# The MLP's second projection waits for each inner tile at the contraction step that reads it, not for all 16 at once

## The chip, the cores and the metric

The kernel runs on one core of a Trainium2 chip. The metric is device time in microseconds (us), the median of three runs. The profiles come from one profiled execution. A core has five engines with their own instruction queues, which are kept in order among each other by semaphores alone: TensorE (PE in the profile, its weight loads PEld), VectorE (DVE), ScalarE (ACT), GpSimd (POOL), and SyncE (SP), which here only issues transfers.

## What is computed

The reference runs one inference step of a 4-layer decoder trunk on 512 prompt tokens and 8 sampled tokens. Each layer has a token mixer (HGRN2, sparse attention, S5, and HGRN2 again) and then a squared-ReLU MLP, each followed by a LayerNorm over the scaled residual. Cut to the MLP, a layer is:

```
FFN_HIDDEN = 4 * D_MODEL          # 1024 -> 4096 -> 1024
def sq_relu_mlp(x, w1, w2):
    return jnp.square(jax.nn.relu(x @ w1)) @ w2
...
xp = layer_norm(DN_ALPHA * xp + mp, ln_mix_g[i], ln_mix_b[i])
xp = layer_norm(DN_ALPHA * xp + sq_relu_mlp(xp, mlp_w1[i], mlp_w2[i]), ln_ffn_g[i], ln_ffn_b[i])
```

The sampled tokens go through the same layers. All arrays are fp32.

## The kernel before

**Layout.** Activations are stored transposed: features on the 128 partitions, the 520 tokens (512 + 8) along the free dimension, in tiles of 128 features by 520 tokens. x has 8 such tiles. Every dense layer is cut into *chunks*: one chunk is a 1024 x 128 block of a weight matrix, that is 8 contraction steps (k) of 128 x 128. To keep fp32 accuracy each operand is split into a high and a low part (x into xh and xl, a weight into wh and wl), and each product is made of three: high by high, low by high, high by low (lines L1476, L1477, L1478 in the function `chunk`). As 520 tokens don't fit one bank of PSUM, each step is done for two halves of 260 tokens. A chunk is thus 8 x 2 x 3 = 48 matmuls of 128*128 by 128x260, each with its own weight load.

**The weight stream.** The weights of the whole program are one stream of 389 chunks. SP loads chunk n into `raw` (2 slots), ACT copies it to `wh` (4 slots, L546 or L554), POOL subtracts to get `wl` (L350) and raises `w_low`. ACT may make the wh of chunk n once PE has finished chunk n-4 (`chunk_done`), so three chunks lie ready ahead of the one in work. In layer 0 the mixer has 40 chunks (numbers 0 to 39); its MLP begins with chunk 40.

**The MLP of a layer** is done in two halves of 16 hidden tiles (HHALF = 16). In each half:

- *First projection*: 16 chunks, one per hidden tile. PE accumulates tile T in one of two PSUM places (`lp`, T % 2). ACT applies ReLU out of PSUM into `lw` (L934, `tile_out`), DVE squares it (L1448), rounds it to the high part `hh` (L1449), and subtracts to get the low part `hl` (L1450). That last one raises `h_ready`, one per hidden tile. `h_ready` counts over the program, and g1 is its value when this half begins.
- *Second projection*: 8 output tiles, each of two chunks (b = 0 and 1), which contract over the 8 hidden tiles 8b to 8b+7. So chunk b reads at step k hidden tile 8b + k. After the second chunk of a tile DVE takes the sum out of PSUM into the residual `r` (L981 in the first half, L979 in the second).

Both projections are loops (`Fori`) of four chunks a pass on PE, except that the first four chunks of the first half are written out, as their steps wait for x tile by tile. The order of instructions on each engine is that of the code. After the second half `stats` (L1505) sums the residual for the LayerNorm (ones_mean).

**Waits on PE at the switch.** Between the two projections PE has one wait, at L1852, for `h_ready >= g1 + 16`: all 16 hidden tiles. Ahead of each tile it waits until the PSUM place is emptied (`tile_out >= T - 1`, the tile before the last), and ahead of each chunk for `w_low`. There are 4 layers x 2 halves = 8 such switches in the program.

Of the kernel before, what the change touches and what calls it, by code (L numbers as in the profile page):

```python
# [26 lines left out]
KT = D // P  # L27
# [8 lines left out]
HHALF = HID // 2 // P  # L36
# [19 lines left out]
SPL = 4  # L56
# [46 lines left out]
def trunk(nc, I, O, kinds=KINDS):  # L103
# [3 lines left out]
    def sb(name, shape, dt=F32, c=ctx):  # L107
        return c.enter_context(nc.sbuf_tensor(name, shape, dt))

    def sem(name):  # L110
        return ctx.enter_context(nc.semaphore(name))
# [29 lines left out]
    hh = sb("hh", [P, HHALF, N], F32R, c)  # L141
    hl = sb("hl", [P, HHALF, N], F32R, c)
# [77 lines left out]
    w_high, w_low, chunk_done = sem("w_high"), sem("w_low"), sem("chunk_done")  # L220
    tile_out = sem("tile_out")
    h_ready = sem("h_ready")
# [1237 lines left out]
    def _(pe):  # L1460
        def bank(T, half):
            b = 2 * (T % 2) + half
            return lp[:, b, 0:NH2]

        def chunk(n, slot, T, hi, lo, k0, start, stop, split=None, ks=range(KT)):

            if 0 in ks:
                pe.wait_ge(w_low, n + 1)
            for k in ks:
                if split is not None:  # L1470
                    pe.wait_ge(xl_ready, split + k + 1)
                w = slice(k * P, (k + 1) * P)
                for half in range(2):
                    t = slice(half * NH2, (half + 1) * NH2)
                    first, last = start and k == 0, stop and k == KT - 1
                    pe.matmul(bank(T, half), wh[:, slot, w], hi[:, k0 + k, t], start=first, stop=False)  # L1476
                    pe.matmul(bank(T, half), wh[:, slot, w], lo[:, k0 + k, t], start=False, stop=False)  # L1477
                    ins = pe.matmul(bank(T, half), wl[:, slot, w], hi[:, k0 + k, t], start=False, stop=last)  # L1478
            return ins

        def tile(n, T, split=None):

            if T >= 2:
                pe.wait_ge(tile_out, T - 1)
            chunk(n, n % SPL, T, xh, xl, 0, True, True, split).then_inc(chunk_done, 1)

        def part(n, T, ks, split=None):

            if 0 in ks and T >= 2:
                pe.wait_ge(tile_out, T - 1)  # L1490
            ins = chunk(n, n % SPL, T, xh, xl, 0, True, True, split, ks)
            if KT - 1 in ks:
                ins.then_inc(chunk_done, 1)

        def pair(n, T, split, ks=range(KT)):

            for k in ks:
                part(n, T, (k,), split)
                part(n + 1, T + 1, (k,), split)
# [235 lines left out]
        for y in plan:  # L1735
# [96 lines left out]
            for half in range(2):  # L1832
                c1, t1 = y["cm"] + 32 * half, y["tm"] + 24 * half
                s0_ = 0
                if half == 0:

                    pair(c1, t1, 8 * (3 * y["i"] + 2))
                    s0_ = 1
                g1 = HHALF * (2 * y["i"] + half)
                if half == 0:  # L1840
                    for c in range(2, 4):
                        tile(c1 + c, t1 + c)
                    lo_, hi_ = 1, HHALF // 4
                else:
                    lo_, hi_ = 0, HHALF // 4
                with pe.Fori(lo_, hi_) as i:
                    for c in range(4):
                        T = t1 + c
                        pe.wait_ge(tile_out, i * 4 + T - 1)
                        chunk(i * 4 + (c1 + c), (c1 + c) % SPL, T, xh, xl, 0, True, True).then_inc(chunk_done, 1)  # L1850
                c2, t2 = c1 + HHALF, t1 + HHALF
                pe.wait_ge(h_ready, g1 + HHALF)  # L1852
                with pe.Fori(0, KT // 2) as i:
                    for m in range(2):
                        T = t2 + m
                        pe.wait_ge(tile_out, i * 2 + T - 1)
                        for b in range(2):
                            n = c2 + 2 * m + b
                            ins = chunk(i * 4 + n, n % SPL, T, hh, hl, 8 * b, b == 0, b == 1)
                            ins.then_inc(chunk_done, 1)  # L1860
# [137 lines left out]
```

## Time and profile before

| what | value |
|---|---|
| median of 3 runs | 3756.96 us (3751.52 to 3760.11) |
| profiled execution, first to last instruction (span) | 3748.7 us |
| PE busy | 3153.9 us, 84% of the span |
| DVE, POOL, ACT busy | 1876.3, 1489.6 and 1120.3 us |
| PE's share of the chain that ended last | 65% |

The profiled execution has no time of its own taken outside the chip's profiler; its span lies 8.3 us below the median of the runs, which also hold the start and the end of the execution. TensorE's granted clock has two levels in this trace: 1.00 of full speed (2.4 GHz) and half of it (1.2 GHz); a value between is a stretch that holds both. In the rows a matmul's end is modelled and neighbours overlap, so the pace is read from start to start.

### The profile page before, as it was taken

How to read it: one execution, taken by the hardware profiler on the slowest of the kernel's cores; microseconds unless marked ns; L12 is line 12 of the kernel's file. 1: busy time of each engine (PE TensorE's matmuls, PEld its weight loads, DVE VectorE, ACT ScalarE, POOL GpSimd, SP SyncE). 2: the span in 40 equal slices, each digit the busy share in tenths (PEclk: the TensorE clock that was granted, in tenths of full speed). 3: DMA queues.
4: the chain of work that ended last, by engine and by line, in shares of the span. 5: the costliest groups of instructions: out<-in, count | busy, mean ns of one | idle time of the engine just before them, and what ended most of it. 6: DMA issues, size and time to landing. Idle time of an engine off the chain costs nothing.

```text
span 3748.7 us, 56136 instructions
## 1 busy us (share of the span) xinstructions
PE 3153.9 (84%) x22360; PEld 2861.9 (76%) x22360; DVE 1876.3 (50%) x2586; ACT 1120.3 (30%) x1827; POOL 1489.6 (40%) x837
## 2 busy tenths in 40 slices
PE   7889689998799788999555667899998888689998
PEld 7888689998589578999511114799998888689997
DVE  4666654252170326233489996460615655754152
ACT  3433332223322223222223222331224433342222
POOL 4222263445233035344345555543443222254443
PEclk9888799999789679999767778999998887899999
DMA  3211122322424212222200000222222212122221
GB/s 113 69 58 58 35 81 85 94 84 68 100 80 155 94 52 79 84 90 84 71 3 1 0 0 12 79 90 84 90 84 72 65 57 58 41 79 85 90 84 68
DMA packets 104309, 260.23 MB, mean 69 GB/s; under 512 B 9587, under 2 KB 44915, under 8 KB 103763
## 3 DMA queue, kind: packets, MB, share of 16 engines
q1 hardware_dynamic: 56592, 206.10, 17.5%
q10 hardware_dynamic: 42434, 34.07, 3.3%
q0 software_dynamic: 5120, 17.83, 1.3%
q8 instruction: 110, 1.80, 0.2%
q14 instruction: 53, 0.43, 0.0%
HBM read 239.09 MB, written 18.88 MB: 69 GB/s over the span
## 4 chain that ended last, share of the span: by engine, by line
PE 65%; DVE 16%; issue 7%; ACT 6%; POOL 3%; DMA 1%; ACTq 1%; DVEq 0%; POOLq 0%; SPq 0%
PE lp L1476 18%; PE lp L1478 17%; PE lp L1477 17%; PE mb L1548 4%; DVE ph L1381 2%; DVE lw L1030 2%; DVE rot L1353 2%; POOL lw L474 1%; DVE lw L1027 1%; DVE dd L1096 1%; PE lp L1705 1%; DVE qt L994 1%; DVE lw L1362 1%; PE mb L1559 1%; PE mb L1648 1%
## 5 line engine op out<-in xcount | busy, mean ns | idle before, releaser
L350 POOL TENSOR_TENSOR wl<-raw,wh 128x1024 fp32r<-128x1024 f32 x389 | 959.6, 2468 | 1449.8 <-ACT wh L554 834.3
L1476 PE MATMUL lp<-xh,wh 128*128 128x260 f32 x4176 | 1238.7, 297 | 101.9 <-POOL xl L360 94.0
L1478 PE MATMUL lp<-xh,wl 128*128 128x260 f32 x4176 | 1212.4, 290 | 0.0
L1477 PE MATMUL lp<-xl,wh 128*128 128x260 f32 x4176 | 1210.8, 290 | 0.0
L1476 PEld LDWEIGHTS lp<-xh,wh 128*128 128x128 f32 x4176 | 823.6, 197 | 115.5 <-issue 79.3
L1477 PEld LDWEIGHTS lp<-xl,wh 128*128 128x128 f32 x4176 | 822.3, 197 | 0.5
L1478 PEld LDWEIGHTS lp<-xh,wl 128*128 128x128 f32 x4176 | 821.2, 197 | 0.0
L1476 PE MATMUL lp<-hh,wh 128*128 128x260 f32 x2048 | 589.1, 288 | 41.0 <-DVE hl L1450 41.0
L1478 PE MATMUL lp<-hh,wl 128*128 128x260 f32 x2048 | 587.6, 287 | 0.0
L1477 PE MATMUL lp<-hl,wh 128*128 128x260 f32 x2048 | 585.9, 286 | 0.0
L1476 PEld LDWEIGHTS lp<-hh,wh 128*128 128x128 f32 x2048 | 395.6, 193 | 42.6 <-POOL wl L350 42.6
L1477 PEld LDWEIGHTS lp<-hl,wh 128*128 128x128 f32 x2048 | 394.9, 193 | 0.0
L1478 PEld LDWEIGHTS lp<-hh,wl 128*128 128x128 f32 x2048 | 394.7, 193 | 0.0
L1791 PE MATMUL lp<-ph,r 128*32 128x512 f32 x256 | 182.5, 880 | 172.9 <-DVE ph L1381 156.5
L1450 DVE TENSOR_TENSOR hl<-lw,hh 128x520 f32 x128 | 315.0, 2461 | 16.4 <-DVE hh L1449 1.2
L546 ACT ACTIVATE wh<-raw 128x1024 fp32r<-128x1024 f32 x192 | 202.7, 1056 | 346.0 <-PE lp L1478 310.6
L1791 PEld LDWEIGHTS lp<-ph,r 128*32 128x32 f32 x256 | 36.2, 154 | 311.2 <-issue 151.7
L554 ACT ACTIVATE wh<-raw 128x1024 fp32r<-128x1024 f32 x197 | 207.1, 1051 | 216.2 <-PE lp L1478 136.7
L981 DVE SCALAR_TENSOR_TENSOR r<-x,lp 128x520 f32<-128x520 f32 x56 | 39.0, 696 | 461.9 <-PE lp L1478 461.8
L1548 PE MATMUL mb<-qt,kt 128*128 128x64 f32 x896 | 171.8, 359 | 106.0 <-ACT tok L692 106.0
L1548 PEld LDWEIGHTS mb<-qt,kt 128*128 128x128 f32 x896 | 169.6, 281 | 109.5 <-issue 109.5
L934 ACT ACTIVATE lw<-lp 128x520 f32<-128x520 f32 x128 | 77.6, 606 | 493.2 <-PE lp L1478 488.9
(307 smaller groups left out, 3713.7 us busy)
## 6 DMA issues: line engine op xcount, KB each, us to landing
raw<-in_wstream SPq DMA_DIRECT2D x389, 512.0 KB, 3.5
s<-in_s_in ACTq DMA_DIRECT2D x16, 512.0 KB, 4.1
out_hg_s<-s ACTq DMA_DIRECT2D x16, 512.0 KB, 3.3
pg<-in_kpages POOLq DMA_DIRECT2D x16, 512.0 KB, 5.7
pg<-in_vpages POOLq DMA_DIRECT2D x16, 512.0 KB, 5.4
bias_rows<-bsm ACTq DMA_DIRECT2D x1, 2560.0 KB
x<-in_xT ACTq DMA_DIRECT2D x4, 520.0 KB, 7.9
out_kT<-r ACTq DMA_DIRECT2D x1, 2080.0 KB, 11.4
```

Source lines behind the costliest of these rows:

```text
L350: pool.tensor_tensor(wl[:, s, :], raw[:, r_, :], wh[:, s, :].bitcast(F32), ALU.subtract).then_inc(w_low, 1)
L546: act.activation(wh[:, s, :], raw[:, r_, :], ACT.Copy).then_inc(w_high, 1)
L554: act.activation(wh[:, n % SPL, :], raw[:, n % RAW, :], ACT.Copy).then_inc(w_high, 1)
L934: act.activation(halves(lw[:, 6 + c % 2, :]), lp[:, 2 * (T % 2):2 * (T % 2) + 2, 0:NH2], ACT.Relu).then_inc(tile_out, 1)
L1030: dve.tensor_tensor(lw[:, 6 + m % 2, :], lw[:, 6 + m % 2, :], rstd, ALU.mult).then_inc(norm_ready, 1)
L1353: dve.tensor_tensor(rot[:, s, a, P:NP_].rearrange("p (a b) -> p a b", b=P), spun[:, 2 * a], spun[:, 2 * a + 1], (ALU.subtract, ALU.add)[a] ...
L1450: dve.tensor_tensor(lo, hq, hi.bitcast(F32), ALU.subtract).then_inc(h_ready, 1)
L1476: pe.matmul(bank(T, half), wh[:, slot, w], hi[:, k0 + k, t], start=first, stop=False)
L1477: pe.matmul(bank(T, half), wh[:, slot, w], lo[:, k0 + k, t], start=False, stop=False)
L1478: ins = pe.matmul(bank(T, half), wl[:, slot, w], hi[:, k0 + k, t], start=False, stop=last)
L1548: ins = pe.matmul(mb[:, 2 if l % 2 else 3, q2], kt[:, l - 1, ct[c]], qt[:, l - 1, q2], start=True, stop=True)
L1791: ins = pe.matmul(lp[f, 1 + k % 2, :], cmat[:, a, t, :], ph[:, t % 2, b, :], start=n == 0, stop=n == 3, tile_position=(0, 32 * (t % 4)))
```

## The change

`chunk` gets an argument `hidden`: where it is given, step k first waits for `h_ready >= hidden + k0 + k + 1`, that is for the hidden tile that it reads (k0 = 8b). The wait for all 16 goes. The first two output tiles of each half (four chunks) are written out ahead of the loop, the first of them with these waits and the second without (hidden=None), and the loop runs over the other six, in three passes.

```diff
-        def chunk(n, slot, T, hi, lo, k0, start, stop, split=None, ks=range(KT)):
+        def chunk(n, slot, T, hi, lo, k0, start, stop, split=None, ks=range(KT), hidden=None):
 
             if 0 in ks:
                 pe.wait_ge(w_low, n + 1)
             for k in ks:
                 if split is not None:
                     pe.wait_ge(xl_ready, split + k + 1)
+                if hidden is not None:
+                    pe.wait_ge(h_ready, hidden + k0 + k + 1)
                 w = slice(k * P, (k + 1) * P)
...
                 c2, t2 = c1 + HHALF, t1 + HHALF
-                pe.wait_ge(h_ready, g1 + HHALF)
-                with pe.Fori(0, KT // 2) as i:
+                for m in range(2):
+                    T = t2 + m
+                    pe.wait_ge(tile_out, T - 1)
+                    for b in range(2):
+                        n = c2 + 2 * m + b
+                        chunk(n, n % SPL, T, hh, hl, 8 * b, b == 0, b == 1, hidden=None if m else g1).then_inc(chunk_done, 1)
+                with pe.Fori(1, KT // 2) as i:
```

No matmul is added, removed or reordered in what is executed, and the programs of DVE, ACT, POOL and SP are the same as before. The first place is PE's program at the switch in the first half of layer 0. In the rows L1846 is the loop of the first projection (L1848 in the changed kernel, whose lines lie two further), L1853 the loop of the second, and in brackets stand the semaphores waited for. Before:

```order
L1478 MATMUL lp<-xh,wl 128x260
L1846 REGISTER_ALU
L1846 COMPARE_AND_BRANCH
L1853 UNCONDITIONAL_BRANCH [waits h_ready]
L1853 ISA
L1468 ISA [waits tile_out]
L1476 MATMUL lp<-hh,wh 128x260 [waits w_low]
L1477 MATMUL lp<-hl,wh 128x260
```

The same place in the changed kernel:

```order
L1480 MATMUL lp<-xh,wl 128x260
L1848 REGISTER_ALU
L1848 COMPARE_AND_BRANCH
L1478 MATMUL lp<-hh,wh 128x260 [waits h_ready,w_low,tile_out]
L1479 MATMUL lp<-hl,wh 128x260
L1480 MATMUL lp<-hh,wl 128x260
L1478 MATMUL lp<-hh,wh 128x260
L1479 MATMUL lp<-hl,wh 128x260
L1480 MATMUL lp<-hh,wl 128x260
L1478 MATMUL lp<-hh,wh 128x260 [waits h_ready]
```

The branch into the second loop and the wait for all 16 tiles are gone from between the projections; the first matmul now waits for the first hidden tile, and each following step (every sixth row) for its own. The second place is where the written-out tiles end and the loop of the second projection begins (L1860 in the changed kernel), four chunks later; before, these rows ran on inside the loop.

```order
L1478 MATMUL lp<-hh,wh 128x260
L1479 MATMUL lp<-hl,wh 128x260
L1480 MATMUL lp<-hh,wl 128x260
L1860 UNCONDITIONAL_BRANCH
L1860 ISA
L1468 ISA [waits tile_out]
L1478 MATMUL lp<-hh,wh 128x260 [waits w_low]
```

The branch into the loop now stands between two chunks, with no wait for the hidden tiles ahead of it. PE's program has 1536 more matmuls in its code (8 switches x 4 chunks x 48), with their weight loads; as the loops make one pass less, as many are executed as before.

## Rows read from the trace of the kernel before

**Rows 1.** The page: busy time, share of the span, instructions; granted clock in 40 slices
```profile
span 3748.7 us, 56136 instructions
PE 3153.9 (84%) x22360; PEld 2861.9 (76%) x22360; DVE 1876.3 (50%) x2586; ACT 1120.3 (30%) x1827; POOL 1489.6 (40%) x837
PEclk9888799999789679999767778999998887899999
```

**Rows 2.** The page's costliest groups: busy us, mean ns; idle before, and releaser
```profile
L1476 PE MATMUL lp<-hh,wh 128*128 128x260 f32 x2048 | 589.1, 288 | 41.0 <-DVE hl L1450 41.0
...
L1476 PEld LDWEIGHTS lp<-hh,wh 128*128 128x128 f32 x2048 | 395.6, 193 | 42.6 <-POOL wl L350 42.6
```

**Rows 3.** The list of waits: us in total, times, longest us
```profile
PE lp L1476 <- DVE hl L1450: 41.0, 8, 5.1
```

**Rows 4.** The timeline at the first switch: start us, us, idle before and releaser
```profile
619.08 0.28 PE L1478 MATMUL lp<-xh,wl 128*128 128x260 f32 x1
619.47 0.60 ACT L934 ACTIVATE lw<-lp 128x520 f32<-128x520 f32 x1 [4.18 <-PE lp L1478]
...
620.11 0.70 DVE L1448 TENSOR_TENSOR lw<-lw 128x520 f32<-128x520 f32 x1 [1.66 <-ACT lw L934]
620.95 0.43 DVE L1449 CAST hh<-lw 128x520 f32 x1
...
621.50 2.63 DVE L1450 TENSOR_TENSOR hl<-lw,hh 128x520 f32 x1
...
624.49 0.58 PE L1476 MATMUL lp<-hh,wh 128*128 128x260 f32 x1 [5.14 <-DVE hl L1450]
```

**Rows 5.** Windows of PE: us, busy us (matmuls), granted clock, DMA share, GB/s
```profile
619.08:624.49 5.41, 0.27 (x3) 0.93 0.28 97
624.49:638.82 14.33, 14.33 (x96) 0.79 0.17 55
...
2719.31:2724.71 5.40, 0.28 (x4) 0.84 0.29 95
2724.71:2738.58 13.87, 13.87 (x97) 0.82 0.20 46
3435.04:3440.44 5.40, 0.28 (x4) 0.94 0.27 95
3440.44:3454.79 14.35, 14.35 (x97) 0.79 0.17 47
```

**Rows 6.** Windows of PE: 15 chunks in mid-loop, and long stretches of one layer's MLP
```profile
719.18:805.28 86.10, 86.10 (x722) 1.00 0.29 91
...
631.00:814.00 183.00, 180.20 (x1507) 1.00 0.28 89
...
524.80:911.50 386.70, 373.57 (x3064) 0.98 0.28 87
```

**Rows 7.** POOL's low parts of weights that had started by 619.1 us
```profile
L350 POOL TENSOR_TENSOR wl<-raw,wh 128x1024 fp32r<-128x1024 f32 x59 | 146.2, 2479 | 336.6 <-ACT wh L554 296.3 <-ACT wh L546 40.2
```

**Rows 8.** PE's timeline: written-out code into a loop, a loop into a loop
```profile
550.20 0.28 PE L1478 MATMUL lp<-xh,wl 128*128 128x260 f32 x1
550.31 0.28 PE L1476 MATMUL lp<-xh,wh 128*128 128x260 f32 x1
...
719.06 0.28 PE L1478 MATMUL lp<-hh,wl 128*128 128x260 f32 x1
719.18 0.28 PE L1476 MATMUL lp<-xh,wh 128*128 128x260 f32 x1
```

**Rows 9.** PE's timeline: a loop into written-out code, and a step with met waits
```profile
910.57 0.28 PE L1478 MATMUL lp<-hh,wl 128*128 128x260 f32 x1
910.69 0.82 PE L1505 MATMUL mb<-lw,ones_mean 128*128 128x260 f32 x3
...
537.75 0.28 PE L1478 MATMUL lp<-xh,wl 128*128 128x260 f32 x1
537.87 0.28 PE L1476 MATMUL lp<-xh,wh 128*128 128x260 f32 x1
```

**Rows 10.** The page's DMA queues: packets, MB, time as a share of 16 engines' span
```profile
q8 instruction: 110, 1.80, 0.2%
```

## The prediction

> **What bounds the kernel now.** I read the page first. PE is busy 84% of the span, and no other engine over half of it [rows 1]. Busy PE is no proof that PE bounds the MLP, so I looked at the long stretches there: in 183 us in the middle of the first layer's MLP the clock is 1.00 throughout, and 15 chunks in the loop take 86.10 us, 5.74 us each or 0.12 us a matmul from start to start, without a gap [rows 6]. In that stretch ACT, POOL and DVE have their chunk's work done and wait for PE. So any time in which PE stands still in the MLP is lost to the span.
>
> The costliest groups then say where it stands still: the 2048 matmuls that begin a step on hh have 41.0 us of idle time before them, released by DVE's hl [rows 2]. The list of waits gives the same as 8 waits of at most 5.1 us, one for each switch [rows 3]. The timeline shows one of them [rows 4]. The last matmul of the last hidden tile starts at 619.08. ACT's ReLU, DVE's square, the rounding and the subtraction follow one after the other, and the subtraction ends at 621.50 + 2.63 = 624.13. PE's next matmul starts at 624.49, 5.41 us after the last one, where 0.12 is the pace. The 0.36 us at the end is semaphore and the branch into the loop.
>
> The reader should see a second loss, which no list of waits shows. After the stall the matmuls run slower: the next two chunks (96 matmuls) take 14.33 us, with a granted clock of 0.79, and two chunks at full pace take 2 x 5.74 = 11.48 [rows 5, 6]. The clock fell to its lower level during the stall, and PE runs the first part of the second projection at it.
>
> **The change, part by part.**
>
> *The wait for 16 tiles goes.* At the switch the first chunk needs hidden tiles 0 to 7 and the second, step by step, 8 to 15. Tile 15 is ready 624.13 - 619.08 = 5.05 us after PE's last matmul starts. PE comes to the step that reads it (k = 7 of the second chunk) after 15 steps of 6 matmuls: 15 x 6 x 0.12 = 10.8 us. Tile 14 was one chunk earlier in everything, so it is ready at about 624.13 - 5.74 = 618.4, before the switch. So each of the 16 new waits is met when PE gets there, the tightest with 10.8 - 5.05 = 5.7 us to spare; DVE's chain would have to more than double before anything is late. What lies beside PE's work is then the same ReLU, square, rounding and subtraction as before. That saves the gap: the eight are 5.41 us once and 5.40 seven times (to 0.01) [rows 5], 43.2 in all, less 8 x 0.12 for the pace, so 42.2 us.
>
> *The clock.* Without the stall, PE goes from one dense stretch into another. In the same trace it goes from the second projection of the first half into the first projection of the second at 719.06 to 719.18, and the clock stays at 1.00 [rows 6, 8]. So I take it that the clock doesn't fall at the switch. The 96 matmuls after the eight stalls took 13.87 to 14.35 us (the shortest and two of the longest are shown [rows 5]); all eight add up to 112.8 us, against 8 x 11.48 = 91.8. That is 21.0 us more to save. The bounds are 0 (the clock falls all the same) and 21.0.
>
> *PSUM and weights, the other two waits at the switch.* Tile t2 needs hidden tile 14 out of PSUM; its ReLU came one chunk before that of tile 15, so at about 613.7. Tile t2 + 1 needs that of tile 15, done at 619.47 + 0.60 = 620.07, when PE is in the first tile until 619.2 + 11.5. Weights: POOL has begun 59 low parts by 619.1 [rows 7], chunks 0 to 58, the last at 615.4, which ends after 2.5 us. The second projection begins with chunk 56; so 56, 57 and 58 are ready, and nothing comes of this wait. The price is 0.
>
> *The new waits as instructions.* A step whose wait is met costs nothing that can be seen: in the first pair of chunks, the second chunk's step at 537.87 waits for an xl tile which the chunk beside it had already used, and starts 0.12 us after its neighbour [rows 9]. Each chunk and each tile in the loop also has waits, and the pace is 5.74 us over 15 of them. I take 0. The upper bound is one start per wait, 16 x 8 x 0.12 = 15 us.
>
> *Written-out code in place of one pass of the loop.* Three seams are exposed now: loop into written-out code, written-out code into the loop, and a longer program to fetch. The first kind costs nothing at 910.57 to 910.69, the second nothing at 550.20 to 550.31, and a loop into a loop nothing at 719.06 to 719.18 [rows 8, 9]. Instructions come in 110 transfers of 16 KB (1.80 MB), whose time is 0.2% of 16 engines' span [rows 10]: 0.002 x 16 x 3748.7 / 110 = 1.1 us each. I take 0, as they run beside 5.74 us chunks; three of them exposed at every switch would be 8 x 3 x 1.1 = 26 us, the upper bound.
>
> The Trainium skill has a rule against this part ("Runtime: NRT & Kernel Launch", section "Instruction fetch mechanics"): a taken branch whose target isn't in the two pages held makes the engine wait for the page to come by DMA. By it, the branch into the second loop, which stood behind the long wait, would now stall PE once a switch, and the sum would shrink; the loop entries of this trace don't show such a stall.
>
> *The sum.* Saved 42.2 + 21.0 = 63.2 us, paid 0. The profiled execution's span of 3748.7 becomes 3685.5. It lies 8.3 us below the median of the runs, which I take over: 3756.96 - 63.2 = 3693.8 us, 1.7% less. DVE takes each output tile out of PSUM right after its second chunk, POOL and ACT are paced by PE's chunks; all move forward with PE, 15.8 us a layer, and the LayerNorm begins that much earlier.
>
> **The rivals.**
>
> *A. The clock falls all the same.* The lower clock could come from the change of operands or from long work instead of the idle time. For it: it follows every switch. Against it: at the switch back, at 719 us, it doesn't fall [rows 6, 8]. Then only the gaps are saved: 3756.96 - 42.2 = 3714.8.
>
> *B. Another wait takes the stall's place, so the change doesn't do what it says.* For it: the weight load at the same place has 42.6 us of idle time put down to POOL's wl, more than the 41.0 of DVE [rows 2]. If chunk 56 really waited for weights, PE would stand as long as before: 3757. Against it: the wl that ended within the stall is that of chunk 59, as 59 others had begun before it [rows 7]; it is named only because it ended last before the release.
>
> *C. Fetching shows.* Three transfers at every switch, 26 us: 3693.8 + 26 = 3720. For it is only that the program grows; the seams [rows 8, 9] speak against it.
>
> *D. Slower: full clock isn't granted for so long.* The longest stretch at 1.00 that I read is the 183 us between two stalls [rows 6]. The MLP of a layer would now be one dense stretch of 386.7 - 15.8 = 371 us. If the stalls are what gives the chip relief, the clock would fall within it. One slow spell costs what one after a stall does, 21.0 / 8 = 2.6 us. The layer gains 15.8 us, so from the seventh spell in a layer on (one every 53 us or closer) the kernel is slower; ten a layer give 3693.8 + 4 x 10 x 2.6 = 3798 us. For it is only that no longer stretch is seen; against it, that the clock is 1.00 right up to the stall after 183 us, with no spell on the way.
>
> The Trainium skill ("TensorE: Matmul & The Clock Gate", the section on the HAM clock gate) names a limiter for the current, which comes with a third busy core of a die and never with one or two. By that rule D falls away here, where one core works; no row of this trace goes beyond the 183 us.
>
> **How the numbers follow.** The forecast has 0.84, A 0.05, B 0.03, C 0.05, D 0.03. The likeliest case has a width of its own: the three runs differ by 8.6 us, 4.3 to each side; and where PE stalls elsewhere (19 of the page's 40 slices have a clock under 9 tenths [rows 1]), everything now comes at other moments, and the clock may return earlier or later, by the 0.5 us between the longest and shortest of the eight [rows 5] in each of the 19, 9.5 us to one side at the most. That is 3680 to 3708. To hold 8 in 10 with A within it I go to 3716. What a measurement can tell from no change is about 0.2%, 7.5 us. Forecast, A and C are faster by more: 0.94; B is no change: 0.03; D slower: 0.03.
>
> **What would show it.** Right, if: the list of waits has no L1478 on hh that waits for DVE's hl; in layer 0 the first matmul on hh starts 0.12 us after the last on xh, at about 619.2; the windows of the next 96 matmuls are 11.48 us at 1.00; the second half's first matmul comes at 719.2 - 7.9 = 711.3; and the clock is 1.00 from 525 us to about 895. A is right if those windows are 14 us after a gap of nothing. B, if the gap is there with POOL or ACT as its releaser. C, if gaps of a microsecond or more stand at L1478 behind the loops, released by nothing. D, if the clock falls in mid-stretch. I'd be wrong most likely in what lies outside the MLP, where I moved everything by 15.8 us a layer and took its length as unchanged.

## The result and the profile after

The changed kernel takes 3694.69 us (median of 4 runs, 3690.57 to 3700.71) against 3755.82 us for the kernel before (4 runs). The ratio is 0.9845 with a 95% interval of 0.9832 to 0.9859. The prediction was 3693.8 us. In the profiled executions the span goes from 3748.7 to 3688.8 us, 59.9 less.

The page's lines that answer to [rows 1, 2, 10]:

```profile
span 3688.8 us, 56096 instructions
PE 3137.7 (85%) x22360; PEld 2847.6 (77%) x22360; DVE 1869.1 (51%) x2586; ACT 1120.4 (30%) x1827; POOL 1491.1 (40%) x837
...
q8 instruction: 123, 2.02, 0.2%
...
L1478 PE MATMUL lp<-hh,wh 128*128 128x260 f32 x2048 | 578.3, 282 | 0.0
...
L1478 PEld LDWEIGHTS lp<-hh,wh 128*128 128x128 f32 x2048 | 385.4, 188 | 0.0
```

PE executes the same 22360 matmuls and is busy 16 us less: 19.5 us less in the four MLPs, where fewer of them run at the lower clock, and 3.3 us more outside them. The idle time ahead of the matmuls on hh was 41.0 us and is 0.0. The 42.6 us that the weight loads at the same place had put down to POOL's wl are gone too. That count belonged to the same stall.

The timeline at the first switch, against [rows 4]:

```profile
623.40 0.28 PE L1480 MATMUL lp<-xh,wl 128*128 128x260 f32 x1
623.52 0.28 PE L1478 MATMUL lp<-hh,wh 128*128 128x260 f32 x1
...
625.83 2.69 DVE L1450 TENSOR_TENSOR hl<-lw,hh 128x520 f32 x1
...
634.30 0.28 PE L1478 MATMUL lp<-hh,wh 128*128 128x260 f32 x1
```

PE goes on after 0.12 us. DVE finishes the last hidden tile at 628.52, beside PE's work. The step that reads this tile begins at 634.30, 5.8 us later. The windows that answer to [rows 5, 6], with length, busy time, matmuls and granted clock:

```profile
623.52:635.01 11.49, 11.49 (x98) 1.00 0.34 105
807.23:818.72 11.49, 11.49 (x98) 1.00 0.33 106
3391.74:3403.23 11.49, 11.49 (x98) 1.00 0.35 110
529.20:907.90 378.70, 370.69 (x3075) 1.00 0.28 89
719.18:805.28 86.10, 86.10 (x722) 1.00 0.29 92
```

Two chunks after a switch take 11.49 us, where they took 13.87 to 14.35. In the first layer the clock is 1.00 from 529.2 us to the end of the MLP at 899.09; only the MLP's first 14 matmuls, right behind the LayerNorm, run at the lower clock, as they did before (run 9). From the fifth chunk of each of the four MLPs on, where its first loop begins, no matmul starts more than 0.13 us after the one ahead of it, the entries into the loops included.

**Where the rest of the difference lies.** The first matmul of the sums for a LayerNorm (ones_mean) marks where a mixer and where an MLP ends. From one such mark to the next, an MLP with the LayerNorm ahead of it took 400.4, 400.3, 405.9 and 400.5 us before and takes 384.5, 384.6, 390.8 and 384.5 now, 62.7 us less in all. All that stands outside these four stretches (mixers, the LayerNorms ahead of them, and the last sums) took 2.8 us more, and 59.9 is left. These are the marks of the first layer: the first row is from the kernel before (its second mark is the 910.69 of [rows 9]), the other two are from the changed kernel.

```profile
510.25 1.91 PE L1505 MATMUL mb<-lw,ones_mean 128*128 128x260 f32 x8
...
514.58 0.60 PE L1507 MATMUL mb<-lw,ones_mean 128*128 128x260 f32 x2
...
899.09 0.38 PE L1507 MATMUL mb<-lw,ones_mean 128*128 128x260 f32 x1
```

Up to 510 us the two kernels have the same instructions on every engine, and yet the changed one's execution was 4.3 us late there. Run 8 looks into whether that is chance. Take these 4.3 us off, and the times named ahead came as written: the first matmul on hh at 623.52 (619.2 forecast), the second half's first matmul at 715.37 (711.3), and the end of the MLP at 899.09 (895).

### The profile page after: what moved, and what is told of

Same layout as the page of the kernel before. It is cut to its first block, busy times and chain, and to the rows that moved or that the text cites. A ratio compares the mean times of both kernels' runs of the same rounds, so it can differ in the third digit from the quotient of the medians.

```text
span 3688.8 us, 56096 instructions
## 1 busy us (share of the span) xinstructions
PE 3137.7 (85%) x22360; PEld 2847.6 (77%) x22360; DVE 1869.1 (51%) x2586; ACT 1120.4 (30%) x1827; POOL 1491.1 (40%) x837
## 4 chain that ended last, share of the span: by engine, by line
PE 65%; DVE 15%; issue 7%; ACT 6%; POOL 3%; DMA 2%; ACTq 1%; DVEq 0%; POOLq 0%; SPq 0%
PE lp L1478 18%; PE lp L1480 17%; PE lp L1479 17%; PE mb L1550 4%; DVE ph L1381 2%; DVE lw L1030 2%; DVE rot L1353 2%; POOL lw L474 1%; DVE lw L1027 1%; DVE dd L1096 1%; PE lp L1707 1%; DVE qt L994 1%; DVE lw L1362 1%; PE mb L1561 1%; PE mb L1507 1%
## 5 line engine op out<-in xcount | busy, mean ns | idle before, releaser
L1480 PE MATMUL lp<-hh,wl 128*128 128x260 f32 x2048 | 578.7, 283 | 0.0
L1478 PE MATMUL lp<-hh,wh 128*128 128x260 f32 x2048 | 578.3, 282 | 0.0
L1479 PE MATMUL lp<-hl,wh 128*128 128x260 f32 x2048 | 576.7, 282 | 0.0
L1478 PEld LDWEIGHTS lp<-hh,wh 128*128 128x128 f32 x2048 | 385.4, 188 | 0.0
L1480 PEld LDWEIGHTS lp<-hh,wl 128*128 128x128 f32 x2048 | 385.2, 188 | 0.0
L1479 PEld LDWEIGHTS lp<-hl,wh 128*128 128x128 f32 x2048 | 385.1, 188 | 0.0
```

## The experiments

Every kernel was timed beside runs of the kernel before on the same chip, so each ratio is to that kernel. Its medians were 3751.99 us beside runs 1, 2, 3 and 5, 3754.23 beside runs 4, 6, 7 and 8, and 3753.42 beside run 9.

**1. Fill the stall, keep the wait.** The kernel before, with extra matmuls ahead of its wait; they compute nothing that is used.

```diff
+                pe.wait_ge(w_low, c2 + 1)
+                for _ in range(42):
+                    pe.matmul(mb[:, 0, 0:NH2], wh[:, c2 % SPL, 0:P], xh[:, 0, 0:NH2], start=True, stop=True)
                 pe.wait_ge(h_ready, g1 + HHALF)
                 with pe.Fori(0, KT // 2) as i:
```

> The kernel before, with its wait for all 16 hidden tiles and its loops, but with 42 extra matmuls of 128*128 by 128x260 at each switch, ahead of that wait (8 x 42 = 336, into a PSUM bank that nothing reads at that time; the outputs are the same). At 0.12 us each they fill 5.0 of the 5.3 us in which PE stands still, so PE's useful work resumes no earlier than before. Theory (the idle time lowers the clock, and the clock's part is worth 21.0 us): the gap stays, the next 96 matmuls take 11.5 us at 1.00, and the time is 3756 - 21 = 3735 us. Rival (the clock falls with the switch of operands or after long work, idle or not): the 96 matmuls keep their 14.1 us and the time stays at 3756. Second rival (some of the 63 us came from the written-out code or its place in the loops): then nothing can be said of it here, as the loops are those of before.

Measured: 3738.49 us, ratio 0.9969 (0.9956 to 0.9983). The windows of its first two switches, gap and then 96 matmuls:

```profile
622.72:628.18 5.46, 5.26 (x45) 1.00 0.26 92
628.18:639.78 11.60, 11.60 (x96) 1.00 0.22 55
811.88:817.36 5.48, 5.27 (x46) 1.00 0.28 96
817.36:828.96 11.60, 11.60 (x97) 1.00 0.20 55
```

PE still goes on with hh 5.5 us after its last matmul on xh, but the chunks behind run at 1.00, at all eight switches. So the clock falls because PE stands idle, not because of the operands or the length of the work. That settles rival A. By the marks, the four MLPs are 19.3 us shorter than in the first profile of the kernel before, and 17.1 shorter than in its second one (run 8). The ratio shows 11.6 us (0.31% of the 3752), with an interval of 6.4 to 16.5. In the profiled execution 7.4 us more lay outside the MLPs; two profiles of the kernel before differ by 4.0 us there, and whether chance or the fillers put the rest there stays open.

**2. Write the code out, keep the wait.**

```diff
                 c2, t2 = c1 + HHALF, t1 + HHALF
+                pe.wait_ge(h_ready, g1 + HHALF)
                 for m in range(2):
...
-                        chunk(n, n % SPL, T, hh, hl, 8 * b, b == 0, b == 1, hidden=None if m else g1).then_inc(chunk_done, 1)
+                        chunk(n, n % SPL, T, hh, hl, 8 * b, b == 0, b == 1).then_inc(chunk_done, 1)
```

> The changed kernel with the written-out first two tiles, but with the old wait for all 16 hidden tiles ahead of them and none at the steps. Theory (the gain is all from the waits, written-out code costs and gives nothing): as before the change, 3756 us, with eight gaps of 5.4 us and a lower clock after each. Rival (the second loop's branch or code fetch plays a part): the 0.36 us between the last hidden tile's low part and PE's first matmul held the branch into the loop; if written-out code is worth something it shrinks, by at most 8 x 0.36 = 2.9 us, to 3753; if it costs one fetch of 1.1 us a switch, 3765.

Measured: 3746.17 us, ratio 0.9982 (0.9970 to 0.9995). The stall stays, so the gain comes from the waits; but it is shorter than before. DVE's last row and PE's next one:

```profile
625.70 2.63 DVE L1450 TENSOR_TENSOR hl<-lw,hh 128x520 f32 x1
...
628.38 0.59 PE L1478 MATMUL lp<-hh,wh 128*128 128x260 f32 x1 [4.83 <-DVE hl L1450]
```

From the tile's end at 628.33 to the matmul are 0.05 us, where it was 0.36 [rows 4]. Before, the wait stood on the branch into the second loop, and the branch was taken only after it. The eight gaps are 5.12 us each and 2.2 us shorter in all. Whether the 0.28 us a switch are the branch itself or the fetching of the loop's code isn't told apart. The slow stretches were shorter as well: the 96 matmuls took 12.92 to 14.29 us and lost 15.6 us in all, where the two profiles of the kernel before lost 21.0 and 18.6. As these two differ by 2.4 us with the same code, it isn't shown that the code shortened the slow stretches. The runs show 6.8 us (1.9 to 11.3). So written-out code behind the old wait is worth something, 2.2 us of it explained by the gaps; the rival of at most 2.9 us lies within the interval.

**3 and 4. Shorter stalls.** Step 4, or step 2, of the first chunk waits for all 16 tiles; the diff for step 4:

```diff
                 if hidden is not None:
-                    pe.wait_ge(h_ready, hidden + k0 + k + 1)
+                    pe.wait_ge(h_ready, hidden + (HHALF if k0 or k >= 4 else k + 1))
```

> The changed kernel, but step 4 of the first chunk waits for all 16 hidden tiles (steps 0 to 3 for their own). PE reaches that step 24 x 0.12 = 2.9 us after the switch and the last tile is ready at 5.05 us, so a stall of some 2.4 us is left of 5.3 (with the 0.25 to 0.3 us that a released wait adds). Theory: the gap costs 8 x 2.4 = 19 us. Whether so short a stall lowers the clock is open: with the clock at 1.00 after it 3695 + 19 = 3714 us; with the same slow spell as after 5.3 us, 3714 + 21 = 3735. If the penalty goes with the length of the stall, half of 21: 3724. I lean to 3714, as in the first layer's MLP of before the pair of chunks has gaps of 1.4 and 2.0 us and the clock is at 1.00 behind them.

> As the run with the wait for all 16 hidden tiles at step 4 of the first chunk, but at step 2, where PE arrives 12 x 0.12 = 1.44 us after the switch. At step 4 the stall was 2.15 us more than the pace, so here 3.6 us. In that run the clock fell at four of eight switches, for one spell of 3.4 us that cost 1.54 us; with the full stall of 5.3 us it fell at all eight, for 6.8 us and 2.6 us lost. Theory (the longer the idle time, the more of the clock is lost): stall 8 x 3.6 = 29 us plus between 8 x 1.5 = 12 and 21 us, so 3695 + 41 to 50 = 3736 to 3745 us. Rival (where the fall comes is a matter of each place and not of the length): four spells again, 6 us, 3730 us.

Measured: 3721.42 us at step 4, ratio 0.9924 (0.9908 to 0.9940); 3745.19 us at step 2, ratio 0.9969 (0.9957 to 0.9981). The stall at step 4, and the windows from the switch to the 97th matmul at the first two switches:

```profile
628.89 0.28 PE L1480 MATMUL lp<-hh,wl 128*128 128x260 f32 x1
631.14 0.39 PE L1478 MATMUL lp<-hh,wh 128*128 128x260 f32 x1 [1.97 <-DVE hl L1450]
...
626.13:639.85 13.72, 11.75 (x98) 1.00 0.27 87
812.08:827.37 15.29, 13.30 (x99) 0.89 0.26 76
```

The stall is 2.25 us from start to start, 2.15 more than the pace, where 2.4 was expected: the released wait added 0.05 us and not 0.25 to 0.3. In each first half the clock stays at 1.00; in each second half it falls behind the stall and costs 1.5 us. At step 2 the stall is 3.7 us, and the clock falls at all eight:

```profile
627.19 0.28 PE L1480 MATMUL lp<-hh,wl 128*128 128x260 f32 x1
630.88 0.59 PE L1478 MATMUL lp<-hh,wh 128*128 128x260 f32 x1 [3.40 <-DVE hl L1450]
...
625.88:643.66 17.78, 14.38 (x98) 0.81 0.22 68
815.88:832.57 16.69, 13.27 (x99) 0.90 0.21 71
```

Summed over the eight windows, step 4 loses 24.3 us (2.15 in each stall and some 7 for the clock) and step 2 loses 45.6 (3.58 in each and 17 for the clock), against 63.2 for the full wait. The medians are 26.7 and 50.5 us over the changed kernel's, and by the ratios, which allow for the chip, it is 30 and 47 us, each uncertain by some 7 us. I leaned to no fall at step 4, which was wrong for half of the switches; at step 2 the forecast of 3736 to 3745 held at its upper end. Whether the clock falls isn't given by the stall's length alone: equal stalls cost 0 or 1.5 us at step 4. Why it is the second halves there isn't shown.

**5. Two coarse waits in the old loop.**

```diff
-                pe.wait_ge(h_ready, g1 + HHALF)
                 with pe.Fori(0, KT // 2) as i:
                     for m in range(2):
...
                         for b in range(2):
+                            if m == 0:
+                                pe.wait_ge(h_ready, g1 + 8 * b + 8)
                             n = c2 + 2 * m + b
```

> The kernel before with its loop of four passes and no written-out code, where the wait for 16 tiles is split in two, ahead of the two chunks of the even output tiles: the first chunk waits for hidden tiles 0 to 7, the second for all 16 (in later passes both are met). PE reaches the second chunk 5.74 + 0.12 = 5.86 us after its last matmul before the switch, and the last hidden tile is ready after 5.05 us, so 0.8 us is left. Theory (a wait met before PE comes costs nothing, and written-out code is not needed): the same as the changed kernel, 3695 us. Rival (waits inside the loop or so small a margin cost): 0.1 us or more at each of 8 x 8 waits, 3701 or more. Second rival (the written-out code had a part in the gain): the same 3701 or more, with the gaps at the loop's start.

Measured: 3695.45 us, ratio 0.9859 (0.9838 to 0.9880), the same as the changed kernel. The first switch (the other seven have the same 11.49 to 11.50 us behind a gap of 0.12) and the number of instruction transfers:

```profile
623.23:634.72 11.49, 11.49 (x98) 1.00 0.33 101
...
q8 instruction: 111, 1.82, 0.2%
```

Neither the 16 separate waits nor the written-out code is needed. One chunk of 5.74 us is enough to cover the 5.05 us of the last hidden tile.

**6. Met waits everywhere.** In the changed kernel every tile of the second projection gets waits at its steps, 896 more.

```diff
-                        chunk(n, n % SPL, T, hh, hl, 8 * b, b == 0, b == 1, hidden=None if m else g1).then_inc(chunk_done, 1)
+                        chunk(n, n % SPL, T, hh, hl, 8 * b, b == 0, b == 1, hidden=g1).then_inc(chunk_done, 1)
...
-                            ins = chunk(i * 4 + n, n % SPL, T, hh, hl, 8 * b, b == 0, b == 1)
+                            ins = chunk(i * 4 + n, n % SPL, T, hh, hl, 8 * b, b == 0, b == 1, hidden=g1)
```

> The changed kernel with a wait at each of the 16 steps of all 8 output tiles, in place of the first tile alone: 8 switches x 7 tiles x 16 = 896 more waits, all met long before. Theory (a met wait costs nothing): 3695 us, and 15 chunks in the loop of the second projection still take 86.1 us. Rival (each costs as an instruction on PE's queue): at half a start, 0.06 us, 54 us more, 3749; at a whole one, 0.12 us, 107 us more, 3802.

Measured: 3693.48 us, ratio 0.9840 (0.9827 to 0.9854). The last 14.5 chunks of the first second projection take 83.24 us, the same 5.74 us each:

```profile
623.07:706.31 83.24, 83.24 (x698) 1.00 0.30 91
```

The four MLPs take 1542.7 us by their marks, against 1544.4 in the changed kernel. So 896 more waits that are met cost nothing that shows.

**7. All tiles written out.** The loop of the second projection goes, and its tiles follow one another.

```diff
-                for m in range(2):
+                for m in range(KT):
                     T = t2 + m
...
-                with pe.Fori(1, KT // 2) as i:
...
```

> The changed kernel with all 8 output tiles of each half written out, so no loop in the second projection: 8 x 12 x 48 = 4608 more matmuls in the code, with their weight loads, and as many executed as before. Theory (fetching is hidden behind 5.74 us chunks): 3695 us, with more instruction transfers in the queue. The old-wait run showed that a branch into the loop behind a wait costs 0.28 us of the gap; here no such branch is on the path, so at most 2 us less. Rival (fetching shows): 123 transfers went to 9216 instructions or so more, so about 36 more; at 1.1 us each 40 us more, 3735.

Measured: 3696.55 us, ratio 0.9842 (0.9826 to 0.9859). There are 146 instruction transfers, 23 more than in the changed kernel. The 36 expected left out that the loop's own four chunks a switch go from the code, so that 8 chunks come on top and not 12; at the 13 transfers that four had brought, that is 26. The pace is unchanged: the next 77.13 us of the same second projection hold no gap.

```profile
621.38:632.87 11.49, 11.49 (x99) 1.00 0.34 104
632.87:710.00 77.13, 77.13 (x648) 1.00 0.31 94
...
q8 instruction: 146, 2.39, 0.3%
```

**8. The kernel before once more.**

> The kernel before once more, unchanged, for a second profile. In the first one the first layer's mixer ended (first sums of the first LayerNorm) at 510.3 us, in the five other profiled kernels, whose programs are the same up to there, at 513.9 to 517.2. Theory (the mixers vary by themselves from one execution to the next, which accounts for the 3 us by which the span fell short of the sum of the switches): it ends at 514 or later here, and the span is 3750 to 3756. Rival (the five kernels have something in common that slows the first mixer): 510 again.

Measured: one run, 3752.19 us, with a span of 3750.5. Its first mark:

```profile
512.61 1.91 PE L1505 MATMUL mb<-lw,ones_mean 128*128 128x260 f32 x8
```

It is not at 514 or later, as I had written, nor at 510 again; the span is within the 3750 to 3756. Over the eleven profiled executions of this case the first mark lies between 505.5 (run 6) and 517.2 us (the run with the wait at step 4), while the program ahead of it is the same in all. So this mixer varies by up to 12 us between executions. The 3 us in question are settled more directly: what lies outside the four stretches from mark to mark took 2145.6 us here, 2141.6 in the first profile of the same kernel, and 2144.4 in the changed one. Over all eleven executions it lies between 2136.3 (run 9) and 2159.4 us (run 4). This profile also shows how much the clock's part varies in the same kernel: the eight gaps are 43.2 us again, but the 96 matmuls after them add up to 110.5 us and not 112.8, so it lost 18.6 us to the clock, where the first profile lost 21.0. Its four MLPs take 1604.9 us, against 1607.1 in the first profile. The windows at the first and the third switch, the longer and the shorter kind:

```profile
626.88:640.96 14.08, 14.08 (x96) 0.80 0.17 44
1537.29:1550.28 12.99, 12.99 (x96) 0.88 0.18 52
```

**9. Keep the clock up after a LayerNorm.** In the changed kernel, ahead of each MLP:

```diff
                 if half == 0:
 
+                    pe.wait_ge(w_low, c1 + 1)
+                    pe.wait_ge(tile_out, t1)
+                    for _ in range(64):
+                        pe.matmul(bank(t1, 0), wh[:, c1 % SPL, 0:P], wh[:, c1 % SPL, 0:NH2], start=True, stop=True)
                     pair(c1, t1, 8 * (3 * y["i"] + 2))
```

> The changed kernel, with 64 extra matmuls of 128x260 in each layer ahead of the MLP's first pair of chunks, where PE stands idle for 8.1 us during the LayerNorm of the mixer; they go to the PSUM place that the pair then starts anew, so the outputs are the same. In the changed kernel's trace the clock is at its lower level from 526.0 to 529.1 us, the pair's first 14 matmuls, as after the old stall. Theory (a low clock costs time only where PE is what is waited for): the pair's steps wait for POOL's xl, with gaps of 1.35 and 2.0 us behind the slow stretch, so the 64 fillers bring the clock back and the gaps grow by as much: the time stays within 2 us of 3695. Rival (the clock's loss counts as at the switch): 14 matmuls at 0.10 us more each, 1.4 us, for 4 layers 5 to 6 us less, 3689; if the fillers run over the idle time, up to 2 us more.

Measured: 3686.73 us, five runs from 3676.21 to 3700.47, ratio 0.9825 (0.9797 to 0.9854). The median is nearer to the rival's 3689 than to 3695, but the interval holds the changed kernel's 0.9845, so the runs don't tell the two apart. The windows of the pair of chunks say more. Here are those of the first three layers, in the changed kernel

```profile
525.99:543.05 17.06, 14.19 (x96) 0.91 0.00 1
1420.64:1437.73 17.09, 15.30 (x97) 0.82 0.00 1
2401.95:2420.40 18.45, 16.22 (x97) 0.79 0.00 1
```

and with the fillers:

```profile
523.08:540.14 17.06, 13.27 (x96) 1.00 0.00 1
1417.83:1434.92 17.09, 13.28 (x97) 1.00 0.00 1
2398.91:2415.99 17.08, 14.28 (x96) 0.90 0.00 1
```

The clock is back, PE's busy time is less, and the pair takes the same 17.06 and 17.09 us, as its steps wait for POOL's xl; in the fourth layer it is the same too. In the third layer it is 1.4 us shorter, but it takes 17.08 us in run 6 as well, which has no fillers, so that isn't shown to be their work. By the marks the four MLPs take 1543.3 us, against 1544.4 without fillers; the rest of the lower time lies outside the MLPs, where nothing was changed. The slow stretch comes from idle time as in run 1, but here it hides under another wait.

## Why the prediction was right

That the time came within 0.9 us is partly luck. The forecast took 63.2 us off a median that was 1.1 us above the later one of four runs, and the medians then lay 61.1 us apart; by the ratio's interval the saving is 53 to 63 us. What the runs confirm is the mechanism and the size of each term to a few us.

- *The wait for 16 tiles, 42.2 us.* Right. The eight gaps went from 5.4 to 0.12 us, and the run with two coarse waits shows that the cover, one chunk against 5.05 us, is real.
- *The clock, 21.0 us.* Right in mechanism. Run 1 shows that idle time is the cause, with the MLPs 19.3 us shorter by it alone. The size was that of one execution: a second profile of the same kernel lost 18.6 us. The term should have had a range of its own, with some 20 us in its middle. Against that second profile the four MLPs of the changed kernel are 60.5 us shorter, not 62.7.
- *PSUM, weights, met waits: 0.* Right. No wait took the stall's place, and 896 more met waits changed nothing. The 42.6 us put down to POOL in [rows 2] went with DVE's wait, which settles rival B.
- *Written-out code: 0.* Right for fetching: 13 and 36 more transfers than before cost nothing that shows, so rival C falls. The Trainium skill's rule on taken branches ("Runtime: NRT & Kernel Launch", section "Instruction fetch mechanics") would have had PE stall at the loop's entry once a switch; the trace doesn't agree, as no step at a loop entry is longer than 0.13 us. What the forecast missed is that code written out behind a wait is worth something when the wait remains: 0.28 us a switch. In the changed kernel that share is contained in the 5.4 us gap, so the sum was not touched.
- *Long stretches at full clock, rival D.* Fell: 378.7 us at 1.00, and the like in the other three layers (365 us at the least).
- *The rest of the program taken as unchanged.* The weakest step. MLPs saved 62.7 us of the 63.2 forecast. The rest took 2.8 us more in the profile, less than the 4.0 us by which two profiles of the kernel before differ there. Of the 8.3 us between span and median of the kernel before, I wrote that they also hold the execution's start and end; in the changed kernel the profiled run took 3690.57 us with a span of 3688.8, so that part is 1.8 us, and the profiled execution was simply one of the shorter ones. Using the same offset for both did no harm, since the sum is a difference.

## What to carry to other kernels

When a consumer waits for all of a producer's tiles, read at which step it needs the last one: a wait in front of that step, or of the chunk that holds it, is enough, and two coarse waits in the loop did here what sixteen and written-out code did. Price a stall of TensorE with what comes after it: here about a third of the gain was in matmuls that ran at the lower clock behind the stall, which no list of waits contains. That second part counts only where PE is what others wait for; behind the LayerNorm the same slow stretch was hidden by POOL, and removing it changed nothing that could be told.

## What was not expected of the hardware

- A wait that stands ahead of a branch into a loop released the first matmul 0.36 us after the producer's end at the first switch and 0.33 at the other seven; the same wait ahead of written-out code released it after 0.05 to 0.06 us.
- Equal stalls don't cost the clock equally. With 2.25 us it fell at four of eight switches, those of the second halves (7 us lost in all), with 3.7 us at all eight (17 us), with 5.1 us at all eight (15.6 us), with 5.4 us at all eight (18.6 and 21.0 us in two executions).
- The first mixer, with the same instructions in every kernel, ended between 505.5 and 517.2 us. On one chip alone (runs 4, 6, 7 and 8) it was 505.5 to 516.9. For a change worth some microseconds, marks inside the trace that enclose the changed part told more than the span did.
